# Projection block: the sample rows' high and low parts in one stationary operand of 64 columns

## The reference, cut to what matters here

```python
z = xn @ p['w_in']                       # xn: normalised rows, D_MODEL = 1024 wide
q = z[..., :ATTN_WIDTH]                  # 768: 12 heads of 64 in 3 groups of 4
k = z[..., ATTN_WIDTH:2 * ATTN_WIDTH]
v = z[..., 2 * ATTN_WIDTH:3 * ATTN_WIDTH]
u = z[..., 3 * ATTN_WIDTH:]              # 256, input of the state space model
q = rope_partial(rmsnorm(q, p['q_norm']), pos) * (HEAD_DIM ** -0.5)
k = rope_partial(rmsnorm(k, p['k_norm']), pos)
```

## Time and profile before

| | |
|---|---|
| three runs, us | 1964.53, 1964.73, 1966.55 (median 1964.73) |
| profiled execution, us | 1968.46 |
| its span, first to last instruction, us | 1966.6 |
| mean granted TensorE clock | 0.949 of full speed |
| TensorE busy | 1813.7 us, 92% of the span |
| VectorE, ScalarE, GpSimd busy | 959.4, 665.7, 249.6 us |

### The profile page before, as it was taken

One profiled execution on the slowest core, in us unless ns is written; L12 is line 12 of the kernel. 1 busy time (PEld: TensorE's weight loads), 2 busy tenths in 40 slices (PEclk: granted clock), 3 DMA queues, 4 the chain that ended last, 5 costly groups with the idle time before them and its releaser, 6 DMA issues. The chain is left out here.

```text
span 1966.6 us, 31339 instructions
## 1 busy us (share of the span) xinstructions
PE 1813.7 (92%) x12419; PEld 1650.8 (84%) x12419; DVE 959.4 (49%) x1929; ACT 665.7 (34%) x1559; POOL 249.6 (13%) x566
## 2 busy tenths in 40 slices
PE   5889999987677898999998989999999999999998
PEld 4888998976454898899677979899899899899896
DVE  6524524546736433644353273545645555454455
ACT  5424324333345322544432053332232223223230
POOL 2511702604412000000000000000000000000000
PEclk9999999985887899899999999999999999999999
DMA  4210110003243532110543103121111212112102
GB/s 149 60 47 31 49 36 26 5 4 113 66 120 89 206 102 92 60 44 2 178 144 97 44 1 89 34 66 33 43 55 33 65 33 63 36 33 66 32 23 89
DMA packets 136239, 125.66 MB, mean 64 GB/s; under 512 B 15722, under 2 KB 128434, under 8 KB 136116
## 3 DMA queue, kind: packets, MB, share of 16 engines
q1 hardware_dynamic: 130500, 109.74, 18.2%
q0 software_dynamic: 5632, 14.44, 2.3%
HBM read 112.79 MB, written 10.70 MB: 63 GB/s over the span
## 5 line engine op out<-in xcount | busy, mean ns | idle before, releaser
L2647 PE MATMUL bank<-XH,WH 128*128 128x352 f32 x1056 | 344.3, 326 | 1.0 <-PEq L1610 1.0
L2647 PE MATMUL bank<-XH,WL 128*128 128x352 f32 x1056 | 341.9, 324 | 0.0
L2647 PE MATMUL bank<-XL,WH 128*128 128x352 f32 x1056 | 341.1, 323 | 0.0
L1967 PE MATMUL bank<-WH,XH 128*128 128x256 f32 x768 | 224.5, 292 | 12.2 <-DVE WL L1834 7.2
L1967 PE MATMUL bank<-WL,XH 128*128 128x256 f32 x768 | 220.4, 287 | 0.0
L1967 PE MATMUL bank<-WH,XL 128*128 128x256 f32 x768 | 219.9, 286 | 0.0
L627 PE MATMUL bank<-WH,XH 128*128 128x256 f32 (+3 forms) x648 | 211.3, 326 | 7.7 <-DVE WL L433 7.7
L2555 DVE TENSOR_TENSOR hres<-hres,bank 128x512 f32<-128x512 f32 (+2 forms) x198 | 135.5, 685 | 158.3 <-PE bank L2680 158.3
L627 PE MATMUL bank<-WL,XH 128*128 128x256 f32 (+3 forms) x648 | 203.0, 313 | 0.0
L627 PE MATMUL bank<-WH,XL 128*128 128x256 f32 (+3 forms) x648 | 202.3, 312 | 0.0
L2647 PEld LDWEIGHTS bank<-XH,WH 128*128 128x128 f32 x1056 | 199.4, 189 | 2.7 <-issue 1.1
(11 more groups left out here) (494 smaller groups left out, 3299.8 us busy)
## 6 DMA issues: line engine op xcount, KB each, us to landing
wstage<-w_up SPq DMA_DIRECT2D x44, 512.0 KB, 5.3
ring<-cache_mem_kv SPq DMA_DIRECT2D x64, 256.0 KB, 4.1
dstage<-w_down POOLq DMA_DIRECT2D x22, 512.0 KB
wstage<-w_in SPq DMA_DIRECT2D x10, 1024.0 KB, 5.1
ringS<-cache_kv_dil SPq DMA_DIRECT2D x16, 512.0 KB, 6.3
wstage<-w_xkv SPq DMA_DIRECT2D x8, 1024.0 KB, 6.5
ringS<-cache_kv_dil SPq DMA_DIRECT2D x48, 128.0 KB, 2.7
xin<-x_prompt SPq DMA_DIRECT2D x8, 512.0 KB, 3.5
```

Source lines behind the costliest of these rows:

```text
L1967: ins = nc.tensor.matmul(MM[s % 3][:r, 0:WB], x[:, k, cols], w[:, b % 2, k], start=k == 0 and i == 0, stop=k == KT - 1 and i == 2)
L2647: ins = nc.tensor.matmul(bank[3 * g + j][:, 0:CH], w[:, slot, k, P * g:P * g + P], x[:, k, CH * j:CH * j + CH], start=k == 0 and i == 0, s ...
```

## The change

In the sample tiles, TensorE multiplies a stationary operand of 64 columns, the high and the low part of the 32 rows side by side, with the high weights, and 32 columns, the high part, with the low weights: 16 matmuls instead of 24. Rows 0 to 31 of the accumulator then hold what belongs to the high part, rows 32 to 63 what belongs to the low part. A new function, `fold_samples`, lets VectorE copy the lower 32 rows to a new tile `zSum` and add the upper ones; in block 2 it does the same first for u, straight into `US`. ScalarE evicts from `zSum` and no longer touches u's sample rows. The low part of the sample rows goes to `XH[:, :, T:T + TS]` instead of `XL`.

```diff
+            def fold_samples(s):
+                b, acc = s // TILES, MM[s % 3]
+                dve.wait_ge(mm, s + 1)
+                if b:
+                    dve.wait_ge(ev, s - TILES + 1)
+                if b == PAIR:
+                    link(nc.vector.tensor_copy(US[:], acc[TS:2 * TS, WB:2 * WB]))
+                    link(nc.vector.tensor_tensor(US[:], US[:], acc[0:TS, WB:2 * WB], ALU.add))
+                nc.vector.tensor_copy(zSum[:], acc[TS:2 * TS, 0:WB]).then_inc(folded, 1)
+                dve.wait_ge(folded, 2 * b + 1)
+                nc.vector.tensor_tensor(zSum[:], zSum[:], acc[0:TS, 0:WB], ALU.add).then_inc(folded, 1)
...
                 if b == 0:
                     prepare(t + 2)
+                if b < BLOCKS and t == NT:
+                    fold_samples(s)
                 if (b, t) in qk_at:
                     sum_squares(qk_at[b, t])
...
                     act.wait_ge(mm, s + 1)
-                    if b == PAIR:
+                    if t == NT:
+                        act.wait_ge(folded, 2 * b + 2)
+                        src = zSum[:]
+                    elif b == PAIR:
...
+                        if t < NT:
+                            xh, xl = columns(XH[:, k], order, t), columns(XL[:, k], order, t)
+                            terms = (xh, WH), (xh, WL), (xl, WH)
+                        else:
+                            terms = (XH[:, k, SEQ:T + TS], WH), (XH[:, k, SEQ:T], WL)
+                            terms = terms if k < KT - 1 else terms[::-1]
```

More of the change, by code:

```diff
@@ L133, in block_project @@
         rl = sb("rl", [P, G * NT, H])
+        zSum = sb("zSum", [TS, WB])
         with ExitStack() as early:
@@ L174, in block_project @@
         zero = sem("zero")
+        folded = sem("folded")
         norm_at = {b * TILES + t + 1: q for q, (b, t) in enumerate(QK)}
@@ L403, in _ @@
                     act.wait_ge(mm, s + 1)
-                    if b == PAIR:
-                        nc.scalar.activation(U[:, :, t] if t < NT else US[:, :].rearrange("p (g h) -> p g h", g=16),
-                                             MM[s % 3][:n, WB:2 * WB].rearrange("p (g h) -> p g h", g=16), ACT.Copy)
+                    if t == NT:
+                        act.wait_ge(folded, 2 * b + 2)
+                        src = zSum[:]
+                    elif b == PAIR:
+                        nc.scalar.activation(U[:, :, t], MM[s % 3][:, WB:2 * WB].rearrange("p (g h) -> p g h", g=16),
+                                             ACT.Copy)
                     nc.scalar.activation(dst, src, ACT.Copy).then_inc(ev, 1)
@@ L447, in prepare @@
                         ks, ts = slice(4 * half, 4 * half + 4), slice(P * (i - 1), P * (i - 1) + n)
-                        nc.vector.tensor_tensor(XL[:, ks, ts],
+                        nc.vector.tensor_tensor(XL[:, ks, ts] if i <= NT else XH[:, ks, T:T + TS],
                                                 TR[half][:, 0:4 * P].rearrange("p (k n) -> p k n", k=4)[:, :, :n],
@@ L622, in _ @@
                             pe.wait_ge(w_lo, CHUNKS * (load + pair) + k // KC + 1)
[L623 to L626, removed]
+                        if t < NT:
[4 more added lines that the diff above has]
+                            terms = terms if k < KT - 1 else terms[::-1]
+                        for j, (x, w) in enumerate(terms):
+                            m = x.shape[-1]
+                            out = MM[s % 3][:m, 0:2 * WB].rearrange("p (a n) -> p a n", a=2) if pair \
+                                else MM[s % 3][:m, 0:WB]
                             ins = nc.tensor.matmul(out, x, w[:, :, k] if pair else w[:, load % 2, k],
-                                                   start=k == 0 and j == 0, stop=k == KT - 1 and j == 2)
+                                                   start=k == 0 and j == 0, stop=k == KT - 1 and j == len(terms) - 1)
                     ins.then_inc(mm, 1)
```

## The result

The change makes the kernel slower, by the mechanism that was forecast, and in the comparison that followed the forecast its time lies above the range.

| comparison | before, median us (runs) | changed, median us (runs) | ratio, 95% interval |
|---|---|---|---|
| first | 1966.55 (5) | 1980.97 (5) | 1.0077, 1.0060 to 1.0095 |
| second | 1968.48 (23) | 1977.95 (6) | 1.0046, 1.0029 to 1.0063 |
| third | 1969.18 (25) | 1979.80 (8) | 1.0061, 1.0040 to 1.0082 |

What follows compares the result with a forecast made beforehand. TensorE was taken to bound the kernel, with 0.95 us of slack in the chain feeding it. Tiles +6.2 us and clock falls +4.5 us, together 10.7 on the median 1964.73, gave 1975.4 us; range 1968.5 to 1980.

Steps and rivals of the forecast that it cites:

- The saved matmuls: 8 of 24 matmuls go in each sample tile: 0.91 us per plain tile, 9.1 us for all nine.
- The drain at a change of tiling mode: Rival: each change of matmul width stops the array, 2.6 us a sample tile; 1983 us; 2 in 100.
- The delay at S0, S3, S6 and S7: Sample (ninth) tiles of blocks 0, 3, 6, 7: queued fold delays eviction; lost 1.3, 1.73, 1.73, 1.42 us.
- S1: Sample tile of block 1: split of u's weights comes late, TensorE starts block 2 later; 2.6 us lost, no slack.
- S1 and S2 had theirs: Sample tiles of blocks 1 and 2 already had their stops, so no new clock falls were counted there.
- S2: Sample tile of block 2, making v and u together: eviction and weight split slightly earlier; gain 0.8 us.
- S4, S5, S8: Sample tiles of blocks 4, 5, 8: first two gain 0.91 us each; at the last the gain goes into a wait, 0.
- the third rival: Clock falls at block 8's sample tile too, wait 0.86 to some 1.8 us; 1977 or 1980 us; 13 in 100.
- The clock: TensorE's granted clock falls after three of four new stops, 1.5 us each: 4.5 us.
- the four new stops: New TensorE stops of 2.3 to 2.6 us at the sample tiles of blocks 0, 3, 6 and 7.
- the sum of 10.7: Whole forecast loss in us: 6.2 from the nine sample tiles plus 4.5 from clock falls.

Runs made afterwards that it cites:

- the idle fold: Kernel before, its 24 matmuls kept, with the fold's two VectorE operations added without effect and ScalarE evicting from zSum; 1.0049, +9.8 us.
- the kernel with three tiles changed: Kernel before with the change in the sample tiles of blocks 2, 4 and 5 alone; 0.9979, then 0.9991.
- the kernel without the fold: Changed kernel with 16 matmuls but no fold, ScalarE evicting rows 0 to 31 from the accumulator, low-part product left out; 0.9979, -4.4 us.
- each repair: Changed kernel with the earlier tile's root, scaling and normalisation first (1.0003), q and k folds on ScalarE and GpSimd (0.9997), or both, block 8 as before (0.9990).

## Why the prediction was right and wrong

**The saved matmuls.** Right: 16 matmuls of S4 take 1.95 us in the changed kernel, and the tile is 0.95 us shorter. TensorE's timeline of the changed kernel at S4:

```profile
245.59 0.36 PE L653 MATMUL bank<-WH,XH 128*64 128x256 f32 x1
245.78 0.28 PE L653 MATMUL bank<-WL,XH 128*32 128x256 f32 x1
...
247.54 0.38 PE L580 MATMUL bank<-ident,zn 128*128 128x128 f32 x2
```

Two widths in turn cost next to nothing here: 0.122 us a matmul, where a plain tile of the kernel before has 0.119. The drain at a change of tiling mode, the rival from the Trainium skill (TensorEngine Tiling (Array Packing), Tiling Modes, Key Properties), is excluded for these two widths by that number.

**The delay at S0, S3, S6 and S7.** Right in mechanism, a little too large: expected 1.3, 1.73, 1.73 and 1.42, found without a fall of the clock 1.4, 1.6, 1.6 and, by the idle fold, 1.0. The eviction is 2.5 us later at S3, S6 and S7 and 2.3 at S0, where 2.67 was worked out.

**S1.** Right as to the delay, and too small as a whole. TensorE starts block 2 at 109.98 instead of 107.31; less the 0.37 by which this execution was late already that is 2.3, where 2.6 was expected. But the step costs 3.4 and 3.5 in two executions and 2.4 in one. The timeline of the changed kernel at S1:

```profile
104.83 0.41 ACT L412 ACTIVATE zs<-zSum 32x256 f32<-32x256 f32 x1 [4.40 <-DVE zSum L471]
...
109.15 2.49 DVE L438 TENSOR_TENSOR WL<-wstage,WH 128x512 fp32r<-128x512 f32 x4
...
109.98 0.79 PE L653 MATMUL bank<-WH,XH 128*128 128x512 f32 x1 [8.45 <-DVE WL L438]
```

The extra is clock, and "S1 and S2 had theirs" was the sentence that failed. Of the first 5.9 us of block 2 the kernel before had 3.2 at the lower level; the first execution of the changed one has the whole. The same at the start of block 3, behind S2. The kernel before, windows behind S1 and S2:

```profile
107.30:113.20 5.90, 5.89 (x19) 5.30 (x20) 1.67 (x3) 0.00 (x0) 0.00 (x0) 0.73 0.58 194
174.70:181.00 6.30, 6.22 (x42) 6.06 (x43) 2.14 (x5) 1.84 (x9) 0.61 (x1) 0.73 0.54 169
```

The changed kernel:

```profile
109.90:115.80 5.90, 5.82 (x14) 4.70 (x15) 1.74 (x3) 0.00 (x0) 0.00 (x0) 0.50 0.58 189
177.90:184.00 6.10, 6.06 (x29) 6.09 (x29) 1.70 (x3) 1.21 (x4) 0.02 (x1) 0.50 0.52 168
```

That the longer stop made the stretch longer isn't shown, and two other executions speak against it. In the second execution of the changed kernel TensorE stood for 8.47 us before block 2 and had 3.4 us of the lower level behind it, about as much as the kernel before; in the second execution of the kernel with three tiles changed, whose S1 is as before, it stood for 5.21 us as before and had it for the whole 5.9. Their windows from the start of block 2, in this order:

```profile
112.00:118.00 6.00, 5.97 (x19) 5.39 (x20) 1.69 (x3) 0.00 (x0) 0.00 (x0) 0.72 0.59 193
107.30:113.20 5.90, 5.87 (x14) 4.71 (x15) 1.70 (x3) 0.00 (x0) 0.00 (x0) 0.50 0.58 190
```

**S2.** The eviction came 0.26 earlier (0.27 was worked out) and block 3 began 0.65 earlier (0.8). Yet the step lost 0.6 in two executions: TensorE stood for 3.64 us instead of 2.46, and the clock took back more than the 0.65, as the second window of either kernel above shows. Where the lower stretch was shorter, 2.9 us instead of 3.4, the step gained even more than the 0.65: 0.9 in the second trace of the kernel with three tiles changed.

**S4, S5, S8.** S4 and S5 are right: 0.9 each; the steps behind S4 take some 5.8 us each, where those behind S3 take 3.1. S8 was counted as 0, and there the third rival came in two of three executions. TensorE's wait behind S8 grew from 0.86 to 1.78 us in all three; the 16 matmuls behind it took 3.23 and 3.32 us at the lower clock in the first and third, and 1.97, as before, in the second. TensorE's timeline in the first and in the second:

```profile
426.00 3.23 PE L623 MATMUL bank<-V,PT 128*128 128x64 f32 x16 [1.78 <-DVE PT L519]
```

```profile
429.46 1.97 PE L623 MATMUL bank<-V,PT 128*128 128x64 f32 x16 [1.78 <-DVE PT L519]
```

Between the last prompt tile and 465 us the three lose 1.0, 0 and 2.8 us more. The same holds over all traces: of six with the wait of 1.78 four had the lower clock right behind it and lost 1.0 to 2.8 us, and the two others lost nothing; none of the six with the wait of 0.8 to 0.9 had it there.

**The clock.** Without it the places come to 1.4 + 2.3 - 0.65 + 1.6 - 0.95 - 0.9 + 1.6 + 1.0 = 5.4 us, where 6.2 were forecast. What is left of the three sums, 4.2, 5.0 and 4.3 us, is put down to the clock; forecast were 4.5, but as three falls behind the four new stops. There were two, three and one, at 1.5 to 1.7 each, and the rest came from the places that were counted as nothing, S1, S2 and elsewhere. That the sum of 10.7 is so near to what all runs give, 11.0, is in part luck: the delay was smaller, the falls were fewer, and S1, S2 and S8 made up for it.

**The step that failed** is then not in the block but in the last line of the sum and in the range. The sum was put on a median of three runs that lay within 2.1 us, 1964.73; the kernel's own median over 76 runs is 1968.9. Of some 5.5 us from the forecast of 1975.4 to the measured 1980.97 this base makes 4.1, the sum 0.3, and the first comparison's five runs lie 1.1 above the median of all 19 of the changed kernel. And the range held only the cases of the block, as if one kernel's executions differed by nothing else. They do, by 14 us for the kernel before and by 18 for the changed one (19 runs, 1972.1 to 1989.7, median 1979.8), and the granted clock goes with it: of the five runs of the first comparison the two slowest, 1986.99 and 1989.66 us, had 0.941 and 0.943, the three others 0.947 and 0.948. In the kernel before it goes with the time less closely: its slowest run, 1976.95 us, had 0.950. There was a hint: the profiled execution, 1968.46, was slower than all three runs. And more than half of what the clock takes lies in the stretch right behind the block, where the change has no part. Two traces show how much that can move one execution: from 465 us to the end, with the same instructions, the second execution of the kernel with three tiles changed gains 7.5 us on the first trace of the kernel before, and the kernel without the fold loses 6.3. The kernel before, windows of the block and of the 385 us behind it (the clock is the third number from the end):

```profile
0.00:465.00 465.00, 404.15 (x2738) 381.08 (x2739) 208.56 (x560) 169.85 (x564) 132.68 (x384) 0.93 0.14 43
465.00:850.00 385.00, 319.17 (x2999) 274.11 (x2999) 211.14 (x468) 158.04 (x334) 79.67 (x115) 0.85 0.36 111
```

The sum on 1968.46 would be 1979.2.

Why the first comparison has 14.4 where the others have 9.5 and 10.6 isn't settled. Its two slow runs have no trace, and five runs a side may just have fallen so: the interval reaches down to 1.0060, and the third's estimate is 1.0061.

**What remains open.** Why a stop of 2.25 us is followed by the lower clock in one execution and not in the next wasn't tried, since no edit sets it. A version with the whole gain of the matmuls (5 us in the block without the fold) was not found: each repair put 0.4 to 1.2 us into another link of the same chain.

## What to carry to other kernels

Before matmuls are saved by adding a step on another engine, look up where that step stands in the engine's queue, and take its start from the instruction ahead of it, not from its input: here a fold of 0.9 us began 2.6 us after its input was complete, and TensorE, whose chain had 0.95 us of slack, paid for it. The experiment that shows it cheaply is the added step without the saving: it cost as much as the whole change, +9.8 us beside +9.5, and its waits, read place by place, tell how much of that is the delay. And when an effect of half a per cent is forecast, take the base and the width of the range from many executions, since three within 2.1 us can lie at one end of a spread of 14.

## What the runs showed of the hardware

An operation of VectorE took twice as long when it started while GpSimd's squares ran. In the changed kernel the same multiplication takes 0.42 us at 219.27 and 0.82 us at 224.68, where GpSimd's squares run from 224.61 to 225.22:

```profile
219.27 0.42 DVE L484 TENSOR_TENSOR zn<-zn,qk_gain 128x256 f32<-128x256 f32 x1 [1.35 <-POOL zn L297]
...
224.61 0.61 POOL L309 TENSOR_TENSOR zsq<-zs 128x256 f32<-128x256 f32 x1
224.68 0.82 DVE L484 TENSOR_TENSOR zn<-zn,qk_gain 128x256 f32<-128x256 f32 x1 [1.72 <-POOL zn L297]
```

It ends 0.28 us after GpSimd does, so it looks held up and not slowed down. In the trace of the kernel before, 9 of the 54 multiplications of this kind started while the squares ran; they took 0.82 to 0.88 us and all ended 0.28 us after the squares. The other 45 took 0.41 to 0.43. The Trainium skill (SBUF — State Buffer, Who interferes with whom) describes that: an operation of VectorE with two inputs in SBUF contends with one of GpSimd that reads SBUF, and which was issued first decides which of them is blocked. The trace agrees as to the order.

The clock's falls are the other surprise: stops of the same length at the same place in the program (2.25 and 2.26 us behind S3) were followed by the upper level in one execution and by 3.4 us at the lower one in another, and a stretch of lower clock that the kernel before has, 3.2 of 5.9 us at the start of block 2, was there for the whole 5.9 in other executions, behind a stop of 8.4 us and behind one of the same 5.21 us as well.
